# Attention scores turned by a product with a diagonal of the reciprocals

## What is computed

```python
scores = einsum('brnqhd,brnkhd->brnhqk', qblk, kblk) * (hd ** -0.5)
scores = where(valid, scores + bias, -inf)
m = max(scores, -1)
e = exp(scores - m[..., None])
s = sum(e, -1)
acc = einsum('brnhqk,brnkhd->brnqhd', e, vblk)
...
outs = [(sd / total)[..., None] * (acc / s[..., None]) for ...]
```

## Time and profile before

| | before |
|---|---|
| median of 3 runs | 1703.47 us (1702.52 to 1705.22) |
| profiled execution, its own time | 1704.5 us |
| its span, first to last instruction | 1702.6 us |
| PE, PEld, DVE, ACT, POOL busy | 1573.0, 1359.3, 677.7, 499.0, 364.2 us |
| mean granted clock of TensorE | 0.967 |

### The profile page before, as it was taken

One profiled execution on the slowest core, in us unless ns is written; L12 is line 12 of the kernel. 1 busy time (PEld: TensorE's weight loads), 2 busy tenths in 40 slices (PEclk: granted clock), 3 DMA queues, 4 the chain that ended last, 5 costly groups with the idle time before them and its releaser, 6 DMA issues. The chain is left out here.

```text
span 1702.6 us, 23488 instructions
## 1 busy us (share of the span) xinstructions
PE 1573.0 (92%) x9228; PEld 1359.3 (80%) x9228; DVE 677.7 (40%) x1188; ACT 499.0 (29%) x951; POOL 364.2 (21%) x387
## 2 busy tenths in 40 slices
PE   5999997999599989969999999999999999995996
PEld 4899996988365668769898988889798888974884
DVE  5402655443365645433232232323222232345664
ACT  4413222343355543332040311204031220313331
POOL 6400004353343422211010100101010110102442
PEclk9999998999799999989999999999999999997999
DMA  7431112341867121122020110202011020312110
GB/s 265 150 107 31 50 56 60 134 119 38 316 235 271 69 94 37 44 62 75 1 74 26 49 49 25 74 0 80 19 49 49 25 74 0 106 44 87 45 43 32
DMA packets 104653, 134.65 MB, mean 79 GB/s; under 512 B 6912, under 2 KB 78528, under 8 KB 104192
## 3 DMA queue, kind: packets, MB, share of 16 engines
q1 hardware_dynamic: 104576, 133.60, 23.5%
HBM read 113.25 MB, written 20.33 MB: 78 GB/s over the span
## 5 line engine op out<-in xcount | busy, mean ns | idle before, releaser
L1532 PE MATMUL ml_U<-h1T_hi,ml_up_hi 128*128 128x364 f32 (+1 forms) x768 | 253.2, 330 | 9.4 <-PE ml_D L1789 4.8
L1532 PE MATMUL ml_U<-h1T_lo,ml_up_hi 128*128 128x364 f32 (+1 forms) x768 | 253.0, 329 | 0.0
L1532 PE MATMUL ml_U<-h1T_hi,ml_up_lo 128*128 128x364 f32 (+1 forms) x768 | 252.7, 329 | 0.0
L1789 PE MATMUL ml_D<-ml_down_hi,ml_u_hi 128*128 128x512 f32 (+1 forms) x576 | 226.2, 393 | 3.1 <-DVE ml_down_lo L1764 2.4
L1789 PE MATMUL ml_D<-ml_down_lo,ml_u_hi 128*128 128x512 f32 (+1 forms) x576 | 224.5, 390 | 0.0
L1789 PE MATMUL ml_D<-ml_down_hi,ml_u_lo 128*128 128x512 f32 (+1 forms) x576 | 224.4, 390 | 0.0
L1716 POOL TENSOR_TENSOR ml_u<-ml_relu 128x364 f32<-128x364 f32 (+1 forms) x96 | 76.2, 793 | 673.7 <-ACT ml_relu L1733 673.7
L1733 ACT ACTIVATE ml_relu<-ml_U 128x364 f32<-128x364 f32 (+1 forms) x96 | 45.6, 475 | 581.8 <-PE ml_U L1532 581.8
L1772 DVE TENSOR_TENSOR R<-R,ml_D 128x512 f32<-128x512 f32 x144 | 98.9, 687 | 265.1 <-PE ml_D L1789 265.0
L1759 DVE TENSOR_TENSOR ml_u_lo<-ml_u,ml_u_hi 128x364 fp32r<-128x364 f32 (+1 forms) x96 | 51.6, 537 | 285.6 <-POOL ml_u L1716 285.6
L1532 PEld LDWEIGHTS ml_U<-h1T_hi,ml_up_hi 128*128 128x128 f32 x768 | 144.9, 189 | 13.0 <-issue 8.2
(11 more groups left out here) (276 smaller groups left out, 2728.9 us busy)
## 6 DMA issues: line engine op xcount, KB each, us to landing
ml_up_raw<-in_w_up SPq DMA_DIRECT2D x32, 512.0 KB, 4.1
ml_down_raw<-in_w_down SPq DMA_DIRECT2D x32, 512.0 KB, 4.6
Kc<-in_cache_kT SPq DMA_DIRECT2D x8, 1536.0 KB, 11.6
Vc<-in_cache_v SPq DMA_DIRECT2D x8, 1536.0 KB, 7.9
fr_raw<-in_w_in SPq DMA_DIRECT2D x16, 512.0 KB, 4.2
in_x<-in_x_prompt SPq DMA_DIRECT2D x8, 512.0 KB, 5.8
h_scratch<-in_h SPq DMA_DIRECT2D x8, 512.0 KB, 3.1
sd_E<-acs_scratch SPq DMA_DIRECT2D x8, 512.0 KB, 3.7
```

The costliest lines, as they stand in the source:

```text
L1532: last = pe.matmul(out, a, b, start=(k == 0 and part == 0), stop=(k == n_k - 1 and part == 2))
L1789: last = pe.matmul(out, a, b[:, f, cols], start=(f == 0 and part == 0), stop=(f == FB - 1 and part == 2))
```

## The change

POOL no longer writes at_Z. For each head of a prompt item it multiplies the identity by the reciprocals and so makes a diagonal matrix at_diag of 128x128, in one of two slots by m % 2. PE turns the blocks of the prompt items by a plain product with that diagonal as the moving operand (Z^T times diag, which is the turned block with every query's column scaled), where it used the transpose with ident. Sample items keep the transpose. Because diag has two slots, POOL waits, from m = 2 on, until the turns of all items up to m - 2 are done. The number of blocks, groups, copies and semaphore counts stays the same; at_diag takes 2 KB more of each partition.

```diff
@@ -1189,6 +1189,7 @@
+    diag = place("at_diag", [P, 2, 2, P])
@@ -1265,11 +1266,12 @@
             for m in range(N):
                 if is_prompt[m]:
-                    n = blocks(m) * P
                     pool.wait_ge(S["inv"], m + 1)
+                    if m >= 2:
+                        pool.wait_ge(S["turn"], group_of[m - 1])
                     for u in range(2):
-                        z = Z[:, m % NZ, u, 0:n]
-                        pool.tensor_tensor(z, z, inv[:, m % NZ, u:u + 1].to_broadcast([P, n]), ALU.mult).then_inc(S["norm"], 1)
+                        pool.tensor_tensor(diag[:, m % 2, u, :], ident[:, :], inv[:, m % NZ, u:u + 1].to_broadcast([P, P]),
+                                           ALU.mult).then_inc(S["norm"], 1)
@@ -1425,7 +1427,9 @@
                     for k in range(min(4, (blocks(m) if is_prompt[m] else NKB) - 4 * g)):
                         kb = 4 * g + k
-                        last = pe.transpose(pT[t % 2][:, k, :], Z[:, m % NZ, u, kb * P:(kb + 1) * P], ident[:, :])
+                        z = Z[:, m % NZ, u, kb * P:(kb + 1) * P]
+                        last = pe.matmul(pT[t % 2][:, k, :], z, diag[:, m % 2, u, :], start=True, stop=True) if is_prompt[m] else \
+                            pe.transpose(pT[t % 2][:, k, :], z, ident[:, :])
```

## The result

The changed kernel takes 1730.74 us (median of 5 runs, 1728.06 to 1733.08) against 1703.47 (5 runs): 27.3 us slower by the medians. The ratio worked out from the single runs is 1.0155, interval 1.014 to 1.017, which makes 26.4 us (24 to 29). The prediction was 1727.5 in a range of 1721 to 1737. The profiled execution has a span of 1728.8 us, 26.2 more than before.

A forecast was written before the change was run, and what follows sets the result against it. The prediction took PE to bound the attention stage: 33.3 us of added PE work, less 5.0 from POOL's stalls and 4.3 absorbed by the copies' stalls, gives 24.0 over the 1703.47 median, so 1727.5 us, range 1721 to 1737.

The forecast's parts named there:

- A turn is one row and a product two: Prompt turns on PE: one row of 0.109 us becomes a plain f32 product of two rows, 2 x 0.112 = 0.224 us.
- 0.115 us more for each block, 33.3 in all: PE, 288 prompt turns: 0.115 us more each makes 33.1 us, corrected for items 0 and 1 to 33.3.
- The first waits: Item 0's 2 turns stand ahead of a 4.5 us wait for Kc, which hides their growth: -0.2 us.
- POOL gives back 5.0: PE's 6.5 us of stalls behind POOL in the attention stage: 5.0 us gained, bounds 3.5 and 6.5.
- The copies take up 4.3: PE's 7.5 us of stalls for ScalarE's at_PT copies, ten items: 4.3 us of the growth absorbed, bounds 3 and 7.5.
- The added wait at nothing: POOL's wait at L1271 for the turns of item m - 2: costed at 0.1 us or less.
- The other signs: Profile: x576 rows near 0.27 us, eight blocks 1.75 to 1.8, POOL x64 at 0.40, PE's waits: POOL below 0.5, at_PT below 3.
- The end passes it on: Next stage, behind a barrier: starts later by attention's growth; nothing there, including PE's 5.0 us weight-split wait, takes any back.
- a product as cheap as a turn: Rival B, prompt turns: a product costs no more than a turn, so the kernel gets faster, 1698.5 us; chance 0.04.
- an open weight load: Rival C, new product rows: loading the weights isn't hidden, 84 us more less 12.5, 1775 us; chance 0.03.
- a product of four turns: Rival D, prompt products: each as long as four turns, 94 us more less 12.5, 1785 us; chance 0.02.
- a hidden cost: Rival E, PE's attention stage: the added work hides in stalls, no change, or partly so at 1706 to 1718; chance 0.03.

The follow-up runs named there:

- the single row of fp32r: Changed kernel with the prompt's exponentials and the diagonals written as fp32r, so both are rounded and a product takes one row: 1702.77 us, ratio 0.9994.
- POOL's half alone: Changed kernel with PE's turns back as transposes with ident; diagonals made and waited for but not read, division left out: 1700.74 us, ratio 0.9977.

## Why the prediction was right

*A turn is one row and a product two*: shown, by x576 in the profile, by the turns issued twice (the price of the rows without a product) and by the single row of fp32r (the product without the price).

*0.115 us more for each block, 33.3 in all*: too low by 2. PE's own pace grew by 35.5 us. The rows step by 0.112 as at L1010, but the first step of each unbroken run is 0.213 us where a turn's was 0.165; the prediction had taken the step of the middle for the whole. Over the middle's step that is 0.101 against 0.056 us, in 43 runs and behind 8 breaks 2.3 us more, and 33.1 + 2.3 = 35.4. (Item 10 with its 0.119 for a block is one of the longest runs; shorter ones pay more for a block.) Nothing in the earlier trace rows could warn of it: the first step at L1010 there is 0.109.

*The first waits*: the prediction took 0.2 us for the growth of item 0, which the wait for Kc hides. The two first waits together took 1.2 us less of the stage than before. That wasn't in the sum; most of it is scatter between executions.

*POOL gives back 5.0*: 5.4 measured by starts in the whole change. POOL's half alone shortens the stage by 4.4 us (3.7 from the first product on Kc), after what the copies take back of it, and the kernel by 3.9 by the ratio. In item 22 the reciprocal is late still: PE shows 0.26 us of idle there behind the diagonal, where the earlier trace rows had 0.74.

*The copies take up 4.3*: 3.6. The interval with five or six blocks became 2.00 us, not 1.85. The timeline of item 9 shows the same chain; ScalarE ends its own work 0.03 us before the copy:

```profile
488.99 1.14 ACT L1362 ACTIVATE at_Z<-at_Z,at_nmax 128x1024 f32<-128x1024 f32 x1
488.99 3.83 PEld L1431 LDWEIGHTS at_T<-at_diag,at_Z 128*128 128x128 f32 x32
488.99 4.02 PE L1431 MATMUL at_T<-at_diag,at_Z 128*128 128x128 f32 x32
...
490.02 0.19 ACT L1362 ACTIVATION_READ_ACCUMULATOR at_Z<-at_Z,at_nmax 128x1 f32 x1
490.25 0.60 ACT L1371 ACTIVATE at_PT<-at_T 128x512 f32<-128x512 f32 x1
...
492.94 1.75 PE L1448 MATMUL at_O<-at_PT,at_V 128*64 128x128 f32 x28
```

The copy starts 1.26 us after the first product (1.25 in items 10 and 14 too, where ScalarE had been idle for 1.2 us, so it is the products that it waits for), where the prediction's four products were complete after 1.05 and the signal took 0.09; the slow first step is 0.10 of the missing 0.12. The 32 rows of both heads take 492.94 - 488.99 = 3.95 us, 2.85 before, so 0.8 of the growth of 1.9 fell into the old stall.

*The added wait at nothing*: shown with four slots. The prediction named a sign for a harmful wait: one at POOL for at_turn that ends with a stall of PE. The rows at 622.43 and 622.97 look just like it, with POOL put down to PE and PE to POOL, and both names are wrong: POOL came 0.08 us behind the reciprocal, PE 0.14 behind the copy.

*The other signs*: x576, POOL's x64 at 0.401 us, eight blocks in 1.78 us from the first row's start to the last's, and waits for at_PT below 3 came true. PE's waits for POOL stand at 0.9 us where the prediction wanted less than 0.5, and are 0.3 without the misnamed one. The mean of a row is 287 ns where about 270 were expected.

*The end passes it on*: PE's first product of the next stage waits 5.00 us for op_w_lo as in the earlier trace rows, and from the end of attention on 0.9 us were added. The sum 35.5 - 1.2 - 5.4 - 3.6 gives 25.3 in the stage against 24.0 predicted; with the 0.9 behind it that is the profile's 26.2. So the mechanism held, and the errors of its terms (2.2 too little for the pace, 0.7 too much for the copies, 0.4 too little for POOL, and the 1.2 of the first waits) partly cancelled, which is luck. The 27.3 of the medians is 1.1 more, the 26.4 of the ratio is not; the changed kernel's own runs lie 5 us apart, so that last microsecond lies within their scatter, and no run here says more of it.

The rivals: a product as cheap as a turn was refuted by the profile; an open weight load (0.2 us a row) and a product of four turns by the step of 0.112 and by the products issued twice; a hidden cost by all of them.

## What to carry to other kernels

Count the rows that an operation makes in the trace before moving work onto the engine that bounds the stage: here a half idle engine was relieved of 48 us for 5, and the full one was charged 35. Where one engine shows waits for another, compare the starts with the same place without a wait; a weight load's idle time, or the name given to a wait for two semaphores, can be far from the price. Where two stages are compared, look at their first waits for data apart; they scatter by themselves. And stalls elsewhere on the same engine are a cover: the copies' stalls took up a tenth of the new work, and would have taken more if the copy's own input had not become late with it.

## What the runs showed of the hardware

- A plain f32 product of 128x128 by 128x128 is two matmul rows with two weight loads of 0.19 us, and costs 0.224 us in a run; a turn is one row with a load of 0.14 us and costs 0.109; an fp32r product of the same shape is one row at about 0.112. The loads are hidden in a run, but the second row of a run comes 0.213 us after the first (turn: 0.165; fp32r product: 0.163).
- A product takes 2.06 times as long as a turn, 0.224 against 0.109 us. The four passes that the Trainium skill states for true FP32 ("FP8 and Floating Point Precision", TensorE Precision Notes) fit that only if a turn is two; no run here counts passes. The factor of four for transpose mode in the Trainium skill's "TensorE: Matmul & The Clock Gate" is not seen in that ratio.
- POOL's instruction with a broadcast operand takes 0.401 us for 128x128 f32 whether it writes in place or into another tile.
